# Hybrid decoder layer on one core: ScalarE's state-space steps one page step later, its unit-row steps ahead of HGRN2 exponentials, and two masks ahead of two scalings

## The reference, cut to what matters

```python
o_a = attend(q, k, v)                       # MoBA: block-sparse attention; samples read a paged cache
o_b, ssm_conv1, ssm1 = mamba2_mixer(...)    # SSM: chunks of 128 tokens
o_c, hgrn1 = hgrn2_mixer(...)               # HGRN2: gated linear attention
o_d, gdn_conv1, gdn1 = gdn_mixer(...)       # gated DeltaNet
mixed = jnp.concatenate([o_a, o_b, o_c, o_d], axis=-1) @ w_out
```

```python
# SSM, per chunk
dec = jnp.exp(jnp.where(mask, acum[:, :, None] - acum[:, None, :], -jnp.inf))
y = einsum(cc, bc, dec, xc) + einsum(cc, h, exp(acum))
# HGRN2: att = einsum('blhk,bshk,blshk->blsh', q, k, exp(where(mask, bcum_l - bcum_s, -inf)))
# gated DeltaNet: unit rows and a masked decay
q = l2_norm(q) * GDN_DK ** -0.5;  k = l2_norm(k)
dec_incl = jnp.exp(jnp.where(incl, gam_l - gam_s, -jnp.inf))
```

## Time and profile before

| what | value |
|---|---|
| median of 3 runs | 1222.05 us (1219.35 to 1226.39) |
| the profiled execution | 1219.89 us, its span 1218.2 us |
| PE busy, PEld busy | 1159.7 us (95%), 1010.1 us (83%) |
| DVE, ACT, POOL busy | 595.1, 449.2, 442.2 us |
| chain that ended last | PE 74%, DVE 13%, issue 4%, ACT 4% |
| mean granted TensorE clock | 0.976 |

### The profile page before, as it was taken

One profiled execution on the slowest core, in us unless ns is written; L12 is line 12 of the kernel. 1 busy time (PEld: TensorE's weight loads), 2 busy tenths in 40 slices (PEclk: granted clock), 3 DMA queues, 4 the chain that ended last, 5 costly groups with the idle time before them and its releaser, 6 DMA issues.

```text
span 1218.2 us, 24817 instructions
## 1 busy us (share of the span) xinstructions
PE 1159.7 (95%) x10272; PEld 1010.1 (83%) x10272; DVE 595.1 (49%) x1056; ACT 449.2 (37%) x802; POOL 442.2 (36%) x370
## 2 busy tenths in 40 slices
PE   7999999988998888999989999989999999999998
PEld 6999997865655578888989657989999999977775
DVE  5699744336479887433291552284343433321003
ACT  6323334245534544234552442462222222221212
POOL 8343433153316110453606000614343434333331
PEclk9999999989979998899999999999999999999999
DMA  5332523066659432247414961503332233232222
GB/s 159 98 87 70 177 62 112 27 192 190 187 146 324 149 108 71 88 125 228 123 34 139 289 205 44 153 3 105 87 87 87 87 87 87 70 105 86 77 80 73
DMA packets 176581, 143.45 MB, mean 118 GB/s; under 512 B 15955, under 2 KB 162820, under 8 KB 176214
## 3 DMA queue, kind: packets, MB, share of 16 engines
q1 hardware_dynamic: 166838, 120.44, 33.3%
q0 software_dynamic: 7200, 20.23, 5.3%
q10 hardware_dynamic: 2432, 1.21, 0.3%
HBM read 131.64 MB, written 10.20 MB: 116 GB/s over the span
## 4 chain that ended last, share of the span: by engine, by line
PE 74%; DVE 13%; issue 4%; ACT 4%; POOL 2%; DMA 1%; SPq 1%; POOLq 0%; DVEq 0%; ACTq 0%
PE PS L264 67%; PE PS L267 7%; DVE SC L704 2%; POOL W_LO L248 2%; DVE PROJ L1942 1%; DVE XN L934 1%; DVE XT L704 1%; DVE PROJ L2363 1%; SPq L534 1%; DVE XN L704 1%; DVE XN_parts L924 1%; ACT PROJ L1345 1%; DVE PROJ L1943 1%; DVE PROJ L704 1%; ACT W_HI L239 0%
## 5 line engine op out<-in xcount | busy, mean ns | idle before, releaser
L248 POOL TENSOR_TENSOR W_LO<-W,W_HI 128x1024 fp32r<-128x1024 f32 x128 | 315.1, 2467 | 617.5 <-ACT W_HI L239 617.4
L264 PE MATMUL PS<-XN_parts,W_HI 128*128 128x272 f32 x1184 | 340.6, 288 | 0.0
L264 PE MATMUL PS<-OM_parts,W_HI 128*128 128x272 f32 x960 | 276.3, 288 | 0.0
L264 PEld LDWEIGHTS PS<-XN_parts,W_HI 128*128 128x128 f32 x1184 | 223.2, 188 | 0.0
L239 ACT ACTIVATE W_HI<-W 128x1024 fp32r<-128x1024 f32 x128 | 134.1, 1053 | 206.6 <-PE PS L264 206.6
L264 PE MATMUL PS<-OM_parts,W_LO 128*128 128x272 f32 x704 | 203.9, 290 | 0.0
L264 PEld LDWEIGHTS PS<-OM_parts,W_HI 128*128 128x128 f32 x960 | 180.7, 188 | 0.2
L264 PE MATMUL PS<-SC_parts,W_HI 128*128 128x272 f32 x608 | 179.0, 294 | 1.9 <-POOL W_LO L248 1.6
L264 PE MATMUL PS<-SC_parts,W_LO 128*128 128x272 f32 x608 | 175.9, 289 | 0.0
L264 PEld LDWEIGHTS PS<-OM_parts,W_LO 128*128 128x128 f32 x704 | 132.3, 188 | 0.0
L264 PEld LDWEIGHTS PS<-SC_parts,W_HI 128*128 128x128 f32 x608 | 114.5, 188 | 5.8 <-issue 3.7
(11 more groups left out here) (406 smaller groups left out, 2067.0 us busy)
## 6 DMA issues: line engine op xcount, KB each, us to landing
W<-in_w_gu SPq DMA_DIRECT2D x44, 512.0 KB, 3.9
W<-in_w_in SPq DMA_DIRECT2D x30, 512.0 KB, 3.8
W<-in_w_down SPq DMA_DIRECT2D x22, 512.0 KB, 3.7
W<-in_w_xkv SPq DMA_DIRECT2D x16, 512.0 KB, 4.1
W_scratch<-in_cache_moba_v SPq DMA_DIRECT2D x36, 128.0 KB, 4.8
W_scratch<-in_cache_moba_v POOLq DMA_DIRECT2D x36, 128.0 KB, 4.9
XT<-in_cache_moba_k SPq DMA_DIRECT2D x32, 128.0 KB, 2.6
XT<-in_cache_moba_k POOLq DMA_DIRECT2D x32, 128.0 KB, 2.5
```

Source lines behind the costliest of these rows:

```text
L248: nc.gpsimd.tensor_tensor(hi_lo(n)[1], raw_chunk(n), hi_lo(n)[0].bitcast(F32), ALU.subtract).then_inc(S("weights_split"), 1)
L264: return nc.tensor.matmul(out, lhsT, rhs, start=start, stop=stop, skip_group_check=True)
```

## The change

Three edits, all in the "ssm" stage.

1. VectorE, levels 4 and 5: the masked decay of the gated DeltaNet is issued ahead of `scaled(6)` and `scaled(7)`, not behind them.
2. ScalarE's own lane order: fifteen times an `m` that stood ahead of four page steps now stands behind the first of them. This moves m0 to m13 and m17 one page step later; all state-space steps with work in them but m16 and m20 are among these.
3. ScalarE's own lane order: where four page steps and a unit step followed an `m`, the unit step now stands ahead of that `m`. So u1 to u5 (and later u7) run ahead of the HGRN2 exponentials of m23 to m27 (and ahead of m28), not behind those of the level before.

TensorE and VectorE keep their lane order. No instruction is added or removed on any engine.

```diff
@@ hgrn_vector
                 if j < H_PACKED or j == 7:
                     placed = place(j, placed)
+                if j in (4, 5):
+                    decay_vector(v, j - 4)
                 if j + 2 < 8:
                     scaled(j + 2)
-                if j in (4, 5):
-                    decay_vector(v, j - 4)
@@ lane orders
+        SCALAR_LANES = LANES.replace("mpppp", "pmppp", 15).replace("mppppu", "umpppp")
+
-        def lanes(main, pages_, unit, norm):
+        def lanes(main, pages_, unit, norm, order=LANES):
             steps = {"m": main, "p": pages_, "u": unit, "n": norm}
-            for lane in LANES:
+            for lane in order:
                 next(steps[lane])
@@ ScalarE
-            stage(s, "ssm", lambda: lanes(mixer_lane(...), moba_sample_scalar(s), unit_scalar(s), ssm_norm_scalar(s)))
+            stage(s, "ssm", lambda: lanes(mixer_lane(...), moba_sample_scalar(s), unit_scalar(s), ssm_norm_scalar(s), SCALAR_LANES))
```

More of the change, by code:

```diff
@@ L3520, in _ @@
                   lambda: [win_parts_scalar(s, k) for k in range(4, KD)], lambda: split_hi(s, NH), lambda: win_scalar(s), enter=False)
-            stage(s, "ssm", lambda: lanes(mixer_lane(s, ssm_scalar(s), hgrn_scalar(s)), moba_sample_scalar(s), unit_scalar(s), ssm_norm_scalar(s)))
+            stage(s, "ssm", lambda: lanes(mixer_lane(s, ssm_scalar(s), hgrn_scalar(s)), moba_sample_scalar(s), unit_scalar(s), ssm_norm_scalar(s), SCALAR_LANES))
             stage(s, "gdn", lambda: gdn_scalar(s), lambda: gdn_lanes(iter(range(11)), mem_scalar(s)), enter=False)
```

## The result

The changed kernel takes 1226.64 us (median of 20 runs, 1224.94 to 1235.02) against 1221.31 us for the kernel before (median of 20, 1219.19 to 1227.69) on the same chips. The ratio is 1.0051, 95% interval 1.0035 to 1.0066: slower by 0.5%; 5.3 us between the medians, 6.2 by the ratio. The forecast was 1222.1 and no change. The time lies inside the range, but it is a loss where I had none, and most of its cause is not in the sum.

A forecast was written before the change was run, and what follows sets the result against it. TensorE, busy 95% of the span, was taken as the bound, so only its waits could win time. Terms -0.9 + 1.5 - 0.5 = +0.1 us gave 1222.1 from the median, no change; range 1217 to 1227.5.

The forecast's parts named there:

- m0: ScalarE's second key tile copied before the table load and gate exponential: TensorE's page step starts earlier, 0.9 us gained (0.4 to 1.8).
- m2, m7, m10: Exponentials and gate step stand between copies one tile later: TensorE stalls equally long, one step later; 0, bounds 0.3 either way.
- m4: Chunk 1's exponentials behind p18's two copies: early TensorE gain, then a wait for VectorE's chunk 0 output; 1.5 us lost.
- The overdraw: VectorE's chunk 0 output shifts 1.43 us against a margin of 0.66 before TensorE's decay rows of chunk 2: 0.8 us over.
- Edits 1 and 3: Levels' tail: earlier masks and unit steps remove waits, but value pages take most back; 0.5 us gained (0.2 to 2.7).
- The floor of the pages: Ahead of u7, full transfer engines keep p103 from starting before about 404.7, so u7 comes at 405.5 to 406.0.
- VectorE's two gains: Levels' tail: VectorE's waits of 1.12 and 1.61 us go, so its tail decay would be done 2.7 us earlier.
- clock stays down: Idle ahead of chunk 2's decay rows keeps the clock at 1.2 GHz for 19 us: +7.1, 1229.2 us; chance 0.08.
- the wait of chunk 2: Sign of right: chunk 2's decay rows on TensorE wait about 2.5 us for VectorE's L2133.
- no wait for L1899: Sign of right: TensorE has no wait for L1899 between 380 and 400 us.
- VectorE's 1.12 gone: Sign of right: VectorE's wait of 1.12 us ahead of L704, at level 5, is gone.
- the clock over 286 to 345: Sign of wrong: granted clock under 0.9 over 286 to 345 us.

The follow-up runs named there:

- all_but_m4: The whole change, except that ScalarE's m4 stays in its old place ahead of the page step: 1225.33 us, ratio 1.0027 to the kernel before.
- m4_only: The kernel before with only ScalarE's m4 moved one page step later: 1226.23 us, ratio 1.0029.
- e2_only: The kernel before with only ScalarE's fifteen m steps moved one page step later: 1227.89 us against 1222.01, ratio 1.0048.
- e3_only: The kernel before with only ScalarE's unit steps moved ahead of the exponentials, VectorE's order as before: 1226.59 us against 1221.56, ratio 1.0049.
- e13: The kernel before with VectorE's masked decay and ScalarE's unit steps moved earlier, the m steps not moved behind a page step: 1228.58 us, ratio 1.0063.
- late_pages: e13 with u7, u8, n1 and m29's work ahead of p101 to p104 on every engine: 1219.72 us, ratio 1.0001 to the kernel before.
- gate_late: The kernel before with VectorE's gate step moved behind the output of chunk 0: 1221.97 us, ratio 1.0006.

## Why the prediction was wrong, by its own steps

- **m0, -0.9: right.** The load at 256.71 waits 0.33 (forecast: under 0.5). Against before, TensorE stands 0.8 us later at 250 us in this trace, before anything was changed, and level at the decay rows of chunk 1 (272.87 against 272.83), so 0.8 was won. It was won by another way than worked out: the load of the table starts 1.4 later than forecast against the rest of the trace, because the two copies stand 0.85 apart (255.96 and 256.81) and not the 0.49 that I took, and a wait of 0.74 is left at 260.37. No run has m0 alone. The table load still takes 1.28 us and the exponential starts 0.01 behind it (257.43 and 258.72).
- **m2, m7, m10, nothing: the stall did move one step, as said** (1.62 us at 271.48, before at 270.50). The clock fell behind it (0.62 for 272 to 281), though behind the same 1.62 us of before it did not, and this trace loses 3.0 us there. In all_but_m4, where m2 moved too, 272 to 281 has 1.00, as in m4_only; e2_only has 0.84. ScalarE's order up to there is the same in the changed kernel, all_but_m4 and e2_only, and all three waited 1.62 us. So I count it as mostly this execution's and not the change's.
- **m4, +1.5 (+0.5 to +2.3): mechanism right, clock term too small.** VectorE's L2092 starts 4.43 later, which is the 3.0 and the 1.43 worked out; the wait for L2133 is 2.92 where 2.5 was said. The stall behind the two copies is 1.48 us (283.51), as the 1.47 of the earlier trace rows foretold. The overdraw accounts for 3.8 - 3.0 = 0.8 of the later start of the decay rows, as forecast. But 58 us on the kernel is 6.4 us late, so 2.6 more is lost behind the wait, at 0.65 for 291 to 300 (below: ScalarE's L2232, first in before, then in the changed kernel). I had 0.7. With 2.6 the term is 3.4, and m4 alone measured 3.5 by the ratio (3.8 in its trace's stretch). That the 2.6 us are the clock's is argued from the 0.65, not tested.

```profile
346.66 0.18 ACT L2232 ACTIVATE SM<-PS 128x16 f32<-128x16 f32 x1 [2.62 <-PE PS L267]
```

```profile
353.07 0.18 ACT L2232 ACTIVATE SM<-PS 128x16 f32<-128x16 f32 x1 [2.62 <-PE PS L267]
```

- **Edits 1 and 3, -0.5 (0.2 to 2.7, all gains): this is the step that failed.** The floor of the pages was seen, and the p101 to p104 waits came (5.3 us; 3 were said), as did VectorE's two gains. What I wrote was that TensorE's wait there only takes the gain back, so that u7 would come at 405.5 to 406.0. But TensorE idled 5.3 us in it, its clock fell, and u7, n1 and level 7, which VectorE waits for, ran at half of full speed. The landing was put too early as well: in e13, where nothing else is late, p103's load starts at 406.20 where 404.7 was said, and u7 at 408.07; why the page lands later is open. In place of -0.5 these edits measured +6.0 (e3_only) and +7.7 (e13); with the idle time filled by matmuls it was +2.1. The bounds had no loss side at all. That the total stayed inside the range is luck: the range was wide for the scatter and for the rivals, and neither had this loss in it.
- **The rival "clock stays down"** had the right kind of loss at one place only, in front of chunk 2, and with 19 us of low clock; there it was some 6 us at the low level (0.65 over 9 us is 0.7 of it at 0.50). The same reasoning applied to edit 3's new waits would have given the sum a loss. The forecast already said that VectorE's wait would move in front of u7; what was missing was to ask what TensorE's clock is when it gets there.
- **The signs.** Of "right": the load at m0, the wait of chunk 2, no wait for L1899, VectorE's 1.12 gone, all came. Page waits came at nearly double. Of "wrong": the clock over 286 to 345 is 0.94, above the 0.9 given.

What stays open: why the losses don't add (5.9 and 7.7 alone, some 6 together). That TensorE, late from m4, comes to the pages later and waits less there is not so: the two page waits sum to 5.3 us in the changed kernel, 5.6 in e13, 5.0 in e3_only and 5.4 in all_but_m4, and the tail stretch is 4.1 to 5.1 us longer in all four. Nor does it explain all_but_m4, at +3.3 against e13's +7.7 with the same tail. The scatter of the times may be enough for it: e13 has 6 runs, and its profiled one is 2.9 below its median where that of all_but_m4 is 3.8 above. No run was made for it. Open too is what e2_only loses behind 348 us.

## What to carry to other kernels

When a step is moved earlier and the engine then meets a transfer that can't come sooner, the price is not zero: look at what runs behind the new idle time and cost it at the low clock. Move the work that someone waits for ahead of the wait (late_pages), and count the slack of every chain through the other engines (gate_late) before moving a step by even one place. Two such mends turned a loss of 0.5% into a gain of 0.2% (0.9956 to 0.9997).

## What was not expected of the hardware

- Idle times of TensorE of 2.9 and of 3.6 with 2.0 us were each followed by stretches at the low level (0.65 over 9 us, 0.50 over 7 to 8 us). Matmuls whose result nobody uses, put in that idle time (14 weight loads in 3.05 us, 0.22 each), kept the clock at 1.00 over 400 to 420 us and made the kernel faster, by 5.6 us by the ratios (2 to 9 by the intervals) and 3.2 in the stretch of the traces. An idle time of 2.08 us (late_pages) was followed by 0.52 over 5 us as well.
- The same idle time of 1.62 us, with the same order on every engine up to there, was followed by a fall in the changed kernel (0.62 for 272 to 281) and not in all_but_m4 (1.00). That is 3.0 us in one execution. The changed kernel's 420 to 460 us ran at 0.83 and before's at 0.96, but gate_late, level with before in its median, had 0.87 there too. So of the 5.6 us by which the two traces differ beyond the medians, 3.0 lie at 272 to 281; the rest is not placed.
